# Two-block expert items: gate and up sums with the expert's weights as the stationary operand

## The reference

```python
xb = u[tok]
gu = xb @ w_gu[e] + b_gu[e]
gate = jnp.minimum(gu[:, :D_FF], SWIGLU_LIMIT)
up = jnp.clip(gu[:, D_FF:], -SWIGLU_LIMIT, SWIGLU_LIMIT)
act = (up + 1) * gate * jax.nn.sigmoid(SWIGLU_ALPHA * gate)
return act @ w_down[e] + b_down[e]
```

## Time and profile before

| | |
|---|---|
| median of 3 runs | 2235.86 us (2235.25 to 2238.87) |
| the profiled execution | 2238.45 us, span of its instructions 2236.4 us |
| TensorE busy | 2161.3 us, 97% of the span |
| VectorE busy | 1698.4 us, 76% |
| ScalarE busy | 1364.3 us, 61% |
| mean granted TensorE clock | 0.98 of full speed |
| moved by DMA | 548.15 MB, mean 245 GB/s |

### The profile page before, as it was taken

One profiled execution on the slowest core, in us unless ns is written; L12 is line 12 of the kernel. 1 busy time (PEld: TensorE's weight loads), 2 busy tenths in 40 slices (PEclk: granted clock), 3 DMA queues, 4 the chain that ended last, 5 costly groups with the idle time before them and its releaser, 6 DMA issues. The chain is left out here.

```text
span 2236.4 us, 34316 instructions
## 1 busy us (share of the span) xinstructions
PE 2161.3 (97%) x10582; PEld 1773.3 (79%) x10583; DVE 1698.4 (76%) x2091; ACT 1364.3 (61%) x1632; POOL 396.6 (18%) x436
## 2 busy tenths in 40 slices
PE   7999999979959999999999999999999999999997
PEld 7987777757848888888888888888888888888884
DVE  5426667776667668879979978679996669997897
ACT  4324665543446556757757756568775557776775
POOL 0000000003331221312212212212220122221121
PEclk9999999989969999999999999999999999999997
DMA  4111101227868667969969969669996669998897
GB/s 163 41 47 34 57 34 43 100 64 208 211 206 294 233 227 281 365 244 367 371 242 367 368 240 332 239 239 383 373 380 242 218 235 334 392 364 316 295 366 288
DMA packets 106509, 548.15 MB, mean 245 GB/s; under 512 B 17911, under 2 KB 28664, under 8 KB 51546
## 3 DMA queue, kind: packets, MB, share of 16 engines
q1 hardware_dynamic: 87850, 504.63, 60.7%
q0 software_dynamic: 18608, 42.85, 8.0%
HBM read 516.18 MB, written 41.47 MB: 249 GB/s over the span
## 5 line engine op out<-in xcount | busy, mean ns | idle before, releaser
L2343 DVE TENSOR_TENSOR wl<-raw,wh 128x2048 fp32r<-128x2048 f32 x423 | 958.5, 2285 | 43.1 <-PE sums L2165 26.8
L2227 ACT ACTIVATE wh<-raw 128x2048 fp32r<-128x2048 f32 x425 | 806.0, 1915 | 92.5 <-DMA raw<-in_w_experts 50.2
L2149 PE MATMUL sums<-wh,xh 128*128 128x512 f32 x1120 | 438.0, 391 | 0.0
L2148 PE MATMUL sums<-wl,xh 128*128 128x512 f32 x1120 | 438.0, 391 | 0.0
L2147 PE MATMUL sums<-wh,xl 128*128 128x512 f32 x1120 | 437.3, 390 | 0.0
L2082 POOL DMA_INDIRECT h_dram<-y,pairs_mine x47 | 121.4, 2584 | 808.9 <-DVE y L2396 485.0
L2148 PEld LDWEIGHTS sums<-wl,xh 128*128 128x128 f32 x1120 | 210.8, 188 | 45.1
L2149 PEld LDWEIGHTS sums<-wh,xh 128*128 128x128 f32 x1120 | 210.8, 188 | 44.7
L2147 PEld LDWEIGHTS sums<-wh,xl 128*128 128x128 f32 x1120 | 211.2, 189 | 43.1
L2147 PE MATMUL sums<-wh,al 128*128 128x512 f32 x560 | 230.2, 411 | 0.6 <-DVE al L2387 0.2
L2149 PE MATMUL sums<-wh,ah 128*128 128x512 f32 x560 | 219.4, 392 | 0.0
(11 more groups left out here) (370 smaller groups left out, 3596.4 us busy)
## 6 DMA issues: line engine op xcount, KB each, us to landing
raw<-in_w_experts SPq DMA_DIRECT2D x426, 1024.0 KB
raw<-in_w_chan SPq DMA_DIRECT2D x20, 512.0 KB, 3.3
o_gate<-in_x SPq DMA_DIRECT2D x8, 512.0 KB, 5.5
raw<-in_w_out SPq DMA_DIRECT2D x8, 512.0 KB, 5.4
ht<-in_x SPq DMA_DIRECT2D x8, 512.0 KB, 8.1
h_dram<-ht SPq DMA_DIRECT2D x8, 512.0 KB
u_dram<-ut SPq DMA_DIRECT2D x8, 512.0 KB
h_all<-h_dram SPq DMA_DIRECT2D x8, 512.0 KB, 7.0
```

The lines of the kernel that those rows point to most:

```text
L2148: pe.matmul(out, hi[:, n, :], w_lo[:, kk, :], start=False, stop=False)
L2149: last = pe.matmul(out, hi[:, n, :], w_hi[:, kk, :], start=False, stop=half == 1 and kk == 3)
L2227: nc.scalar.activation(wh[ch % HIGHS][:, :, :], raw[ch % RAW][:, :, :], ACT.Copy).then_inc(h_split.sem, 1)
L2343: dve.tensor_tensor(wl[ch % LOWS][:, :, :], raw[ch % RAW][:, :, :], wh[ch % HIGHS][:, :, :], ALU.subtract).then_inc(l_split.sem, 1)
```

## The change

In two-block items the gate and up sums are made the other way round: a 128 x 128 tile of weights is the stationary operand, and the item's 192 tokens move. The sums then have features in rows. For each chunk TensorE goes through the 4 steps of the contraction and, in each, through the chunk's 4 tiles of 128 columns (2 of gate, 2 of up). Two products are made with each tile: the high weights with high and low tokens together (384 columns), and the low weights with the high tokens (192 columns). The down projection is as before, and so are one-block items.

- The activations come out with features in rows, so a two-block item has no `turn_act`. They are split from SBUF.
- The bias is a column value that VectorE adds; the bias products of two-block items go. A new table `b_columns` (256 KB) and a split-off `pick_consts` (16 KB) are loaded behind `blank`, and `small_loaded` counts 96 in place of 64.
- Each gate or up pair of tiles takes two banks. There are six banks in a ring of three pairs: `sums` (two pairs) and `a_ps`.
- ScalarE copies the low tokens' sums (columns 192 to 383) out, VectorE adds the others and the bias, then clamps.
- In each item ScalarE rounds one chunk fewer ahead (chunk 4 moves behind the second block's split), and so does VectorE (chunk 2). The second block's tokens are turned and split in two halves, before chunk 0's products begin.

```diff
+        xx = sb("xx", [P, KT, 2, 2 * P], F32R)
+        xh, xl = xx[:, :, 0, 0:P], xx[:, :, 1, 0:P]
...
+        ring = [k.sums[:, 0:2, :], k.sums[:, 2:4, :], a_ps[:, :, :]]
...
+            def begin_sums(i, g, blocks):
                 if g < 2:
                     pe.wait_ge(y_read.sem, y_read.at(i, g - 1))
+                elif blocks == 2 and g == 4:
+                    pe.wait_ge(gate_ready.sem, gate_ready.at(i, 4))
                 else:
                     pe.wait_ge(gu_read.sem, gu_read.at(i, g - 1))
...
+            def tile_free(i, g, j):
+                if g == 0:
+                    pe.wait_ge(y_read.sem, y_read.at(i, j // 2 - 1))
+                elif (g, j // 2) in ((1, 1), (2, 1), (3, 1)):
+                    pe.wait_ge(gate_ready.sem, gate_ready.at(i, g))
+                elif g > 1:
+                    pe.wait_ge(gu_read.sem, gu_read.at(i, g - 1))
+
+            def by_weights(i, ch):
+                g, half = GROUP_OF[ch], HALF_OF[ch]
+                pe.wait_ge(*low_done(i, ch))
+                w_hi, w_lo = wh[ch % HIGHS], wl[ch % LOWS]
+                for kk in range(4):
+                    n = half * 4 + kk
+                    for j in range(4):
+                        if n == 0 and j % 2 == 0:
+                            tile_free(i, g, j)
+                        out = ring[(2 * g + j // 2) % len(ring)][:, j % 2, :]
+                        own = slice(j * P, (j + 1) * P)
+                        pe.matmul(out[:, 0:2 * ROWS].rearrange("p (a b) -> p a b", b=ROWS), w_hi[:, kk, own], xx[:, n, :, 0:ROWS],
+                                  start=n == 0, stop=False)
+                        last = pe.matmul(out[:, 0:ROWS], w_lo[:, kk, own], xx[:, n, 0, 0:ROWS], start=False, stop=n == KT - 1)
+                        if n == KT - 1 and j == 1:
+                            last.then_inc(gates_made.sem, 1)
+                last.then_inc(parts_used.sem, 1)
...
             def item(i, blocks):
                 pe.wait_ge(x_low.sem, x_low.at(i, 0))
                 if blocks == 2:
                     pe.wait_ge(xg_loaded[1].sem, xg_loaded[1].at(i, 16))
-                    turn(1)
+                    for half in range(2):
+                        turn(1, range(4 * half, 4 * half + 4))
+                    for ch in range(8):
+                        if ch < 2:
+                            pe.wait_ge(x_low.sem, x_low.at(i, ch + 1))
+                        by_weights(i, ch)
...
+            def copy_low(i, g, part):
+                if g == 0 and part == 0:
+                    act.wait_ge(y_read.sem, y_read.at(i, 0))
+                if part == 0:
+                    act.wait_ge(gates_made.sem, gates_made.at(i, g + 1))
+                    to = tg[:, 0:2 * ROWS].rearrange("p (a b) -> p a b", b=ROWS)
+                else:
+                    act.wait_ge(parts_used.sem, parts_used.at(i, LAST_CHUNK[g] + 1))
+                    to = uc[:, 0:2 * ROWS].rearrange("p (a b) -> p a b", b=ROWS)
+                sums = ring[(2 * g + part) % len(ring)][:, :, ROWS:2 * ROWS]
+                nc.scalar.activation(to, sums, ACT.Copy).then_inc(low_copied.sem, 1)
...
+            def clamp_tiles(i, g):
+                dve.wait_ge(low_copied.sem, low_copied.at(i, 2 * g + 1))
+                for j in range(2):
+                    last = fold(g, j, tg[:, j * ROWS:(j + 1) * ROWS])
+                last.then_inc(second_ready.sem, 1)
+                dve.wait_ge(second_ready.sem, second_ready.at(i, 2 * g + 1))
+                t = tg[:, 0:2 * ROWS]
+                dve.tensor_scalar(t, t, LIMIT, None, ALU.min).then_inc(gate_ready.sem, 1)
+                dve.wait_ge(low_copied.sem, low_copied.at(i, 2 * g + 2))
+                for j in range(2):
+                    last = fold(g, 2 + j, uc[:, j * ROWS:(j + 1) * ROWS])
+                last.then_inc(gu_read.sem, 1)
...
             def item(i, blocks):
                 if blocks == 2:
-                    low_second(i)
+                    low_second(i, 0)
+                    low_second(i, 1)
+                    dve.wait_ge(sel_ready.sem, sel_ready.at(i, 1))
+                low(i, 2)
                 low(i, 3)
...
             sp.dma_start(blank[:, :], k.d["unused"]).then_inc(small_loaded.sem, 16)
+            sp.dma_start(k.b_columns[:, :, :], k.d["b_columns"]).then_inc(small_loaded.sem, 16)
+            sp.dma_start(k.pick_cons[:, :], k.d["pick_consts"]).then_inc(small_loaded.sem, 16)
             sp.wait_ge(blanks.sem, blanks.at(0, 2))
-            sp.wait_ge(small_loaded.sem, small_loaded.at(0, 64))
+            sp.wait_ge(small_loaded.sem, small_loaded.at(0, 96))
```

More of the change, by code:

```diff
@@ L2110, in _, with turn @@
             pe.sem_inc(parts_used.sem, parts_used.credit)
-            def turn(b):
-                for n in range(KT):
+            def turn(b, tiles):
+                for n in tiles:
                     last = pe.transpose(x_ps[:, n, :], xg[b][:, n * P:(n + 1) * P], k.c["ident"])
@@ L2126, in turn_act @@
                 last.then_inc(act_turned.sem, 1)
-            def biases(i, g, blocks):
+            def begin_sums(i, g, blocks):
                 if g < 2:
                     pe.wait_ge(y_read.sem, y_read.at(i, g - 1))
+                elif blocks == 2 and g == 4:
+                    pe.wait_ge(gate_ready.sem, gate_ready.at(i, 4))
                 else:
                     pe.wait_ge(gu_read.sem, gu_read.at(i, g - 1))
-                for b in range(blocks if g < 4 else 0):
-                    pe.matmul(acc[g % 2][b][:, :], sel[:, b, :], bias[:, g * 512:(g + 1) * 512], start=True, stop=False)
+                if g < 4:
+                    pe.matmul(acc[g % 2][0][:, :], sel[:, :], bias[:, g * 512:(g + 1) * 512], start=True, stop=False)
@@ L2158, in second_block @@
                     n = half * 4 + kk
[L2159 to L2165, removed]
+                    pe.matmul(out[:, :], ab[:, n, :], w_lo[:, kk, :], start=n == 0, stop=False)
+                    last = pe.matmul(out[:, :], ab[:, n, :], w_hi[:, kk, :], start=False, stop=half == 1 and kk == 3)
                 return last
@@ L2169, in products @@
                 if HALF_OF[ch] == 0:
-                    biases(i, GROUP_OF[ch], blocks)
+                    begin_sums(i, GROUP_OF[ch], blocks)
                 last = first_block(i, ch)
@@ L2179, in item @@
                     pe.wait_ge(xg_loaded[1].sem, xg_loaded[1].at(i, 16))
-                    turn(1)
-                else:
[L2182 to L2195, removed]
+                    for half in range(2):
[4 more added lines that the diff above has]
+                        by_weights(i, ch)
+                else:
+                    pe.sem_inc(x_turned.sem, 2)
+                    pe.sem_inc(gates_made.sem, gates_made.per)
+                    pe.wait_ge(sel_ready.sem, sel_ready.at(i, 1))
+                    for ch in range(8):
+                        products(i, ch, blocks)
+                        if ch >= 3 and ch % 2 == 1:
+                            turn_act(i, (ch - 3) // 2)
                 pe.wait_ge(a_low.sem, a_low.at(i, 2))
@@ L2320, in _ @@
             act.wait_ge(x_turned.sem, x_turned.at(0, 0))
-            copy_x(0).then_inc(x_high.sem, 1)
-            for ch in range(1, HIGHS - 1):
+            copy_x().then_inc(x_high.sem, 1)
+            for ch in range(1, HIGHS - 2):
                 high(0, ch)
@@ L2567, in lay_out @@
                        for g in range(4)] + [bd[:, g * 512:(g + 1) * 512] for g in range(2)], axis=1)
+    columns = biases[:, 0:4].reshape(N_EXPERTS, 4 * 4, P).transpose(2, 1, 0)
     return {
@@ L2579, in lay_out @@
         "router_w": ca(feature_tiles(x["router_w"][0])), "router_b": ca(x["router_b"][0]),
-        "w_experts": ca(experts), "b_experts": ca(biases), "final_g": ca(x["final_g"]),
+        "w_experts": ca(experts), "b_experts": ca(biases), "b_columns": ca(columns), "final_g": ca(x["final_g"]),
     }
```

222 lines of the change are left out of this document (115 added, 107 removed).

## The result

The changed kernel takes 2298.5 us (median of 4, 2296.4 to 2301.9) against 2235.6: the ratio is 1.0268, 95% interval 1.0247 to 1.0288. It is slower by 63 us, where 26 were forecast and 2284 was the upper end of the range. It was forecast to be slower and is slower, but by more than twice what was forecast.

The account below looks back on a forecast made before the run. TensorE was taken as the bound, an item lasting as long as its products. 7 x 1.3 + 5 x 2.2 + 7 x 0.65 + 1.0 gave some 26 us more: 2262 against the median, range 2245 to 2285.

Parts of the forecast that it names:

- Part 1: Gate and up products of two-block items: 128 pairs at 284 ns replace 168 products, 36.4 us against 38.1.
- first rival: Weight loads hidden beside the 384-column product: 264 ns a pair, 2234 us in all; chance 0.27.
- third: Rival: a narrow F32R product is as slow as plain float32, 508 ns a pair, about 2600 us; chance 0.07.
- Parts 2 and 3: Two-block items: 16 of 32 turnings go, saving 1.8 us; TensorE's waits for ring banks cost 4.0 us an item.
- list of products: A two-block item without waits takes 56.3 us, 3.9 below 60.2; over 12 items 47 us less.
- ring's waits: TensorE waits for `gate_ready` before reusing banks: 0.85 us three times and 1.45 once with restarts, 4.0 us an item.
- second rival: Waits cost nothing while a pair costs 284 ns: 47 us less, 2190 us; chance 0.03.
- Part 4: Start of a two-block item: TensorE waits for the second block's split, 2.1 us behind a two-block item, 1.2 behind a one-block.
- Part 5: One-block items behind two-block ones start with splits left over: 0.65 us longer each, bounds 0 to 1.5.
- Part 6: Loading 272 KB more of tables behind `blank` lies wholly on the path: 1.0 us, bounds 0 to 2.

Follow-up runs that it names:

- e6: Changed kernel with a reordered four-pair ring and chunk 0 in two passes, the first needing only the first block: 2220.1 us, ratio 0.9924.
- e4: Changed kernel with the low weights' product over 128 columns in place of 192: 2300.6 us, ratio 1.0283.
- e9: Changed kernel with the low weights' product over 256 columns in place of 192, the extra ones zeros: 2311.2 us, ratio 1.0305.
- e8: Changed kernel with a reordered four-pair ring and the second block's tokens not split, their columns zeros: 2202.1 us, ratio 0.9849.
- e2: Changed kernel with the tokens' bank pair x_ps added as fourth pair of the ring: 2247.9 us, ratio 1.0045.
- e1: Changed kernel with nine unread 512-column products between the turnings and chunk 0 of every two-block item: 2285.6 us, ratio 1.0206.
- e7: Kernel before the change, with TensorE's wait for the second block's split moved ahead of chunk 0 in two-block items: 2302.2 us, ratio 1.0290.
- e3: Changed kernel with the second block's tokens turned but not split, their columns zeros, chunk 0 not waiting for them: 2259.1 us, ratio 1.0088.
- e5: Changed kernel with both the fourth ring pair x_ps and the nine unread products before chunk 0: 2233.0 us, ratio 0.9976.

## Why the prediction was wrong

**Part 1, the unknown price: right.** 112 ns were taken for the 192-column product from two rows of other products, and a pair came out at 286 ns for 284. e6, e4, the changed kernel and e9 show the floor by width: 128 with 192 columns 223, 384 with 128, 192 and 256 columns 288, 286 and 294. That it is the weight load was forecast from the earlier trace rows; the runs show a floor of 111 ns a product at 128 and 192 columns, and do not show that the load sets it. The Trainium skill, "TensorE: Matmul & The Clock Gate", section "LDWEIGHTS (loading the stationary operand)", gives a load as its columns divided by 1.2, so 107 ns for 128 columns of weights; the trace's 111 is 4 ns above it. The first rival (264 ns, loads hidden) and the third (508 ns) are out.

**Parts 2 and 3: right.** The list of products is 56.36 us in e8 for 56.3. The ring's waits came to 0.8 three times and 1.4 once, and their removal made an item 4.1 us shorter, where 4.0 were forecast. The second rival (waits cost nothing) is out.

**Part 4, the head: the step that failed, and in two ways.** The first is its size. The prediction counted the instructions between the last product and the split, durations and hand-overs only, and left out that a loop's end, a load and a branch stand there, at which VectorE now idles for 0.76 us and ScalarE for 1.23. The wait is 2.9 and 2.3 us instead of 2.1 and 1.2, 7 x 1.1 + 5 x 0.8 = 12 us in all; the items of e2 (44.8 and 44.2 us) less those of e8 (41.87) give the same 2.9 and 2.3. No row of the trace of before shows this idle time, since a weight split lay over it.

The second is the clock. The prediction took every product at 2.4 GHz, because the items of before ran at 1.00 throughout. It forecast a wait of 1 to 2 us for TensorE in every two-block item and put nothing down for what such a wait does to the clock. Eleven stretches of 3.4 us at the 1.2 GHz level followed, 1.6 us each: 17.6 us by the items' lengths, and 13 in e1's median.

**Part 5, the neighbours: mis-sized.** A one-block item behind a two-block one took 0.65 us longer in the forecast. The seven stretches from a two-block item's last turnings to the next took 294.2 us, for 289.5 before, although four turnings of activations had gone from each. These were worth 0.68 us, as the stretch from a two-block item's last turnings to the own turnings of another two-block item shows, 15.17 us before and 14.49 now, with the same other products in it. So the neighbours lost 9.5 us, 1.4 each. In the changed kernel's timeline TensorE waits for VectorE's `av`, which came late behind a split:

```profile
1383.85 2.31 DVE L2389 TENSOR_TENSOR wl<-raw,wh 128x2048 fp32r<-128x2048 f32 x1
...
1387.03 0.42 DVE L2447 SCALAR_TENSOR_TENSOR av<-uc,tg 128x256 f32<-128x256 f32 x1 [0.21 <-DVE uc L2410]
...
1387.51 0.44 PE L2139 MATMUL a_ps<-cons,av 128*128 128x128 f32 x2 [1.24 <-DVE av L2447]
```

It is not the waits of the two-block item, since the seven stretches are as long in e8, which has none of them (294.4 us). That the split left for later is the cause is argued from such rows; no run puts it back.

**Part 6, the tables: not told apart.** VectorE now waits 1.5 us for `pick_cons` where it waited 1.9 for `blank`, and the first turning starts at 643.1 us for 642.4. In the profiled executions of the experiments it starts between 640.5 and 648.7, so 1 us cannot be seen.

**The sum.** By the lengths of the stretches in the traces, in us over all items:

| term | forecast | shown |
|---|---|---|
| list of products | -47 | -46 |
| ring's waits | 48 | 49 |
| waits at the head | 19 | 31 |
| half clock behind the head | 0 | 18 |
| neighbours | 5 | 9.5 |
| tables | 1 | not told apart |
| sum | 26 | 62 |

The items are 61 us longer in the profiled executions, the whole 63 in the medians. The clock, put at nothing, and the head's size are 30 of the missing 37 us. The range was too narrow even for the prediction's own bounds: with 6 us for the ring, 3 for the head, 1.5 for a neighbour, 2 for the tables and 290 ns a pair its sum is 57 us above the middle, 2319, and it gave 2285 without a reason. No bound stood for the clock.

## What to carry to other kernels

An engine that bounds the kernel and never idled has a cover at every seam, and a reordering that takes the cover away must be charged for the wait, for what the engines that end it do between two items, and for the clock behind it. A new formulation can be better in its list of work and worse in its waits: run it once with the waits taken out (e8, -1.5%), and it is then known what an edit against the waits can win. Two edits of that kind, a bank pair that was idle at the time and sixteen products that need the first block alone, made ahead of the wait, turned +2.7% into -0.8%.

## What was not expected of the hardware

In the changed kernel the clock fell, in 8 of 11 cases, 0.7 to 1.3 us after TensorE had gone back to work, in the other three within 0.3 us of its return; so the products that run slowly are mostly not those next to the idle time.

The same idle time may or may not cost the 1.6 us. Four traces have the same heads, idle for 2.1 us in seven of them and for 2.7 in five: the half clock followed in 11 of 12 (the changed kernel), 10 (e4), 7 (e2) and 6 (e9). In e7 it followed all five idle times of 3.9 us and two of the seven of 3 us. Idle times of 0.6 to 0.8 us (e1, e3, e6) were followed by none. In e2, e4, e5, e6 and e9 one stretch lies in a one-block item, each time behind 1.9 to 2.4 us of waiting for `av`. So two executions of one kernel can differ by several us for this reason alone.

The recorded starts of alternating products of different widths (198 and 88 ns, or 228 and 60) do not tell each product's cost: they moved between the changed kernel and e4 while the pair's distance stayed within 2 ns.
